# The last stage of a fused two-block transformer kernel: four places for split operands, and gates and gelus loaded in double pairs

## The chip, the cores and the metric

One core of a Trainium2 chip (trn2) runs the whole program. The metric is the device time in microseconds (us), the median of several runs. TensorE (PE) multiplies, VectorE (DVE), ScalarE (ACT) and GpSimd (POOL) do the elementwise work, SyncE (SP) issues most transfers, and 16 DMA engines move the data between the chip's memory and SBUF.

## The reference, cut to what matters

The reference is a chain of two transformer blocks over 512 tokens of width 1024. All but the end of the second block is untouched by the change. That end is a layer of 16384 small experts (`peer_ffn`): each token picks 8 x 16 experts, and its output is the sum of their rows of `v`, each weighted by a gelu of the token's product with the expert's row of `u` and by a gate.

```python
def peer_ffn(h, w_q, keys1, keys2, u, v):
    ...
    def chunk(args):
        h_c, e_c, g_c = args
        a = jnp.einsum('cd,ced->ce', h_c.astype(jnp.float32), u[e_c].astype(jnp.float32))
        act = jax.nn.gelu(a, approximate=False) * g_c
        return jnp.einsum('ce,ced->cd', act, v[e_c].astype(jnp.float32))
    ...
x = x + peer_ffn(rmsnorm_2(x, norm2_g[l]), w_peer_q[l], peer_keys1[l], peer_keys2[l],
                 peer_u[l], peer_v[l])
```

## The kernel before

**Two ways for the experts.** For 384 of the 512 tokens (TD = 384) the kernel takes no picks: it multiplies by all experts, with a gate of zero where a token has not picked one. The 16384 experts are 64 pairs (PAIRS) of 256, 2 x 128 each. In the stage before the last, the products with `u` are made, their gelu goes to DRAM (`gelu_dram`, 384 KB a pair), and the gates, built from one-hot products, go to `gates_dram`. The other 128 tokens go by gathers: 128 gathers (SLOTS) of rows of `v`, two a pair, which GpSimd issues and VectorE multiplies by a scalar and adds into two PSUM banks (`add_rows`, line 1849).

**The last stage.** For each pair p it computes out[384 tokens, 1024] += (gelu x gate)[256 experts, 384] transposed, times v[256 experts, 1024]. Multiplications keep float32 precision with operands that are split into a high half (rounded to fp32r) and a low half (the rest): high x high, low x high, high x low. So a pair is 2 (halves of its experts) x 3 (token blocks) x 2 (512 columns) x 3 = 36 matmuls of 128 x 128 by 512 (lines 906 to 908, `outputs_of`), added up in six PSUM banks over all 64 pairs.

**Who does what for pair p.**
- SP issues the loads: a slab of weights of 1 MB into one of two places of `raw` (`value_slab`, line 374, when the slab two before it is split), then the gelus (line 384) and the gates (line 386) of the pair into one of two places (`pair`, when the product two before is out). All go through one queue; the gathers have another.
- ACT makes the high half of the weights, `W_hi<-raw` (`high`, line 1330), when PE is through with the pair that had the place, p-2, and the high half of the operand, `B_hi<-arena` (`operand`, line 1337), for which there are two places as well.
- GpSimd makes the low half of the weights, `W_lo<-raw,W_hi` (`low_of`, line 408), and then issues two gathers (line 464); gather k has one of eight places, and waits until VectorE has added the row block of gather k-8.
- VectorE does, in this order: the product gelu x gate (`product_of`, line 1830), the two sums of pair p-2 (`add_rows`), the low half of the operand, `B_lo` (`low_of`, line 1839).
- PE waits for `slab_split` (the low half of the weights) and `act_lo_ready` (the low half of the operand), and releases places with `slab_used`.

The engines are in step through semaphores alone; each runs its own list in the order in which it was written. The counts that are waited for are multiples of the pair: `slab_used` counts all slabs since the start, so that `slab_used >= slab - 1` means that the slab two before is through. At the end the four blocks of 128 tokens are copied out of PSUM by ACT and VectorE in turn (`x_done`) and stored. The block of the gathered tokens is copied first, when all its sums are made.

## Time and profile before

| what | value |
|---|---|
| median of 3 runs | 2793.13 us (2790.08 to 2794.68) |
| profiled execution | 2801.39 us, its span 2799.6 us |
| TensorE clock granted, mean over the span | 0.964 of full |
| PE busy | 2585.7 us (92%) |
| GpSimd busy | 1798.3 us (64%) |
| VectorE busy | 1674.6 us (60%) |
| ACT busy | 726.0 us (26%) |
| DMA, mean over the span | 180 GB/s, 502.83 MB |
| last stage, first to last matmul | 2221.3 to 2793.6 us of the span |

The span runs from the first to the last instruction; the profiled execution is some 8 us longer than the median of the timed runs. A busy share over the whole span says little here, since the stages have different limits; the stretch from 2221 us on is the one that the change touches. Matmuls overlap in the records, so their pace is the distance between two starts, not the duration of one. Rows of the timeline give an instruction's start, its duration, and in brackets how long its engine had been idle before it and who ended that.

### The profile page before, as it was taken

To read this page: it belongs to the slowest core of one execution; us is meant where nothing else is said; L and a number is where in the kernel's file an instruction comes from. 1 tells how busy PE (TensorE), PEld (TensorE's weight loads), DVE (VectorE), ACT (ScalarE), POOL (GpSimd) and SP (SyncE) were. 2 spreads that over 40 slices of the span, in tenths; PEclk is the share of its full clock that TensorE was granted. 3 is DMA by queue.
4 is the path that set the end of the run, shared out by engine and by line. 5 is a ranking of instruction groups with operands and counts; after the bars stand their busy time and mean duration, and the time that the engine had idled before them with its cause. 6 is when DMAs were issued, how large, how long until landed. Compare 5 with 4: busy or idle time off the path is not lost.

```text
span 2799.6 us, 36306 instructions
## 1 busy us (share of the span) xinstructions
PE 2585.7 (92%) x12764; PEld 2159.1 (77%) x12764; DVE 1674.6 (60%) x3128; ACT 726.0 (26%) x1296; POOL 1798.3 (64%) x1315
## 2 busy tenths in 40 slices
PE   4989799999899998998889989999999999999998
PEld 2866578888686675677778889999999977777777
DVE  5457531111334224454449998878788388878887
ACT  4158310000222323433311011111112123322332
POOL 2746557676651252375656568998986778777786
PEclk8989899999998998999999999999999999999999
DMA  6224222222210011122123336899997899989897
GB/s 239 90 83 151 91 75 95 101 90 97 104 61 31 31 60 49 46 91 91 63 95 111 119 123 253 310 351 327 350 333 260 317 324 325 329 298 324 314 327 256
DMA packets 160500, 502.83 MB, mean 180 GB/s; under 512 B 12288, under 2 KB 79488, under 8 KB 128896
## 3 DMA queue, kind: packets, MB, share of 16 engines
q1 hardware_dynamic: 96432, 311.98, 31.8%
q0 software_dynamic: 36864, 134.23, 12.9%
q10 hardware_dynamic: 27088, 55.11, 5.2%
q8 instruction: 68, 1.11, 0.2%
q14 instruction: 48, 0.39, 0.0%
HBM read 448.84 MB, written 52.43 MB: 179 GB/s over the span
## 4 chain that ended last, share of the span: by engine, by line
PE 58%; DVE 13%; POOL 10%; DMA 9%; issue 5%; ACT 4%; SPq 0%; ACTq 0%; DVEq 0%; POOLq 0%
PE banks L546 8%; PE banks L548 8%; PE banks L547 8%; POOL W_lo L408 6%; DMA arena<-gates_dram 5%; PE banks L676 3%; PE banks L906 3%; PE banks L907 2%; PE banks L908 2%; PE banks L821 2%; PE banks L823 2%; PE banks L822 2%; PE banks L694 2%; PE banks L652 2%; PE banks L695 2%
## 5 line engine op out<-in xcount | busy, mean ns | idle before, releaser
L408 POOL TENSOR_TENSOR W_lo<-raw,W_hi 128x2048 fp32r<-128x2048 f32 x127 | 586.6, 4619 | 58.8 <-ACT W_hi L1330 53.2
L433 POOL TENSOR_TENSOR W_lo<-raw,W_hi 128x512 fp32r<-128x512 f32 x376 | 493.8, 1324 | 0.0
L436 POOL TENSOR_TENSOR beat<-zero 128x1 f32<-128x1 f32 x94 | 19.3, 205 | 650.8 <-PE banks L696 255.8
L821 PE MATMUL banks<-A_hi,W_hi 128*128 128x384 f32 x1024 | 380.3, 371 | 18.9 <-ACT B_plain L1258 17.9
L823 PE MATMUL banks<-A_hi,W_lo 128*128 128x384 f32 x1024 | 345.3, 337 | 0.0
L822 PE MATMUL banks<-A_lo,W_hi 128*128 128x384 f32 x1024 | 344.3, 336 | 0.0
L906 PE MATMUL banks<-W_hi,B_hi 128*128 128x512 f32 x768 | 306.2, 399 | 33.3 <-DVE B_lo L1839 33.3
L907 PE MATMUL banks<-W_hi,B_lo 128*128 128x512 f32 x768 | 304.6, 397 | 0.0
L908 PE MATMUL banks<-W_lo,B_hi 128*128 128x512 f32 x768 | 304.1, 396 | 0.0
L546 PE MATMUL banks<-A_hi,W_hi 128*128 128x512 f32 x680 | 265.8, 391 | 4.9 <-issue 4.9
L548 PE MATMUL banks<-A_hi,W_lo 128*128 128x512 f32 x680 | 264.7, 389 | 0.0
L547 PE MATMUL banks<-A_lo,W_hi 128*128 128x512 f32 x680 | 264.6, 389 | 0.0
L428 POOL CAST W_hi<-raw 128x512 fp32r<-128x512 f32 x376 | 248.5, 675 | 0.0
L821 PEld LDWEIGHTS banks<-A_hi,W_hi 128*128 128x128 f32 x1024 | 195.4, 191 | 20.7 <-issue 12.1
L906 PEld LDWEIGHTS banks<-W_hi,B_hi 128*128 128x128 f32 x768 | 147.6, 192 | 70.5 <-DVE B_lo L1839 39.3
L464 POOL DMA_INDIRECT arena<-v_rows,arena x128 | 158.3, 1237 | 66.3 <-DVE banks L1849 43.2
L1839 DVE TENSOR_TENSOR B_lo<-arena,B_hi 128x768 fp32r<-128x768 f32 x64 | 190.5, 2977 | 11.9 <-ACT B_hi L1337 11.8
L822 PEld LDWEIGHTS banks<-A_lo,W_hi 128*128 128x128 f32 x1024 | 195.6, 191 | 0.0
L823 PEld LDWEIGHTS banks<-A_hi,W_lo 128*128 128x128 f32 x1024 | 193.8, 189 | 0.0
L416 POOL CAST W_hi<-raw 128x2048 fp32r<-128x2048 f32 x65 | 123.7, 1904 | 108.5 <-PE banks L823 86.6
L1330 ACT ACTIVATE W_hi<-raw 128x2048 fp32r<-128x2048 f32 x62 | 118.7, 1914 | 281.3 <-PE banks L908 281.2
L1830 DVE TENSOR_TENSOR arena<-arena 128x768 f32<-128x768 f32 x64 | 132.2, 2066 | 79.4 <-DMA arena<-gates_dram 79.3
(259 smaller groups left out, 5541.6 us busy)
## 6 DMA issues: line engine op xcount, KB each, us to landing
raw<-weights SPq DMA_DIRECT2D x241, 1024.0 KB, 4.9
gelu_dram<-B_plain ACTq DMA_DIRECT2D x64, 384.0 KB
gates_dram<-arena ACTq DMA_DIRECT2D x48, 512.0 KB, 9.1
arena<-gelu_dram SPq DMA_DIRECT2D x64, 384.0 KB, 7.6
arena<-gates_dram SPq DMA_DIRECT2D x64, 384.0 KB, 10.2
W_plain<-weights SPq DMA_DIRECT2D x4, 1024.0 KB, 15.7
X<-x_t SPq DMA_DIRECT2D x1, 2048.0 KB, 14.3
arena<-v_rows,arena POOLq DMA_INDIRECT x128, 8.4
```

The source lines that it names most:

```text
L408: pool.tensor_tensor(W_lo[:, s % 2, :], raw[:, s % 2, :], W_hi[:, s % 2, :].bitcast(F32), ALU.subtract)\
L428: pool.tensor_copy(W_hi[:, j, cols], raw[:, j, cols]).then_inc(slab_half, 1)
L433: return pool.tensor_tensor(W_lo[:, j, cols], raw[:, j, cols], W_hi[:, j, cols].bitcast(F32), ALU.subtract)
L546: mm(to, lh, rh, start=i == 0, stop=False)
L547: mm(to, lh, rl, start=False, stop=False)
L548: last = mm(to, ll, rh, start=False, stop=i == n - 1)
L821: mm(to, lh, rh, start=k == 0, stop=False)
L822: mm(to, lh, rl, start=False, stop=False)
L823: last = mm(to, ll, rh, start=False, stop=k == KD - 1)
L906: mm(to, lh, rh, start=False, stop=False, skip_group_check=True)
L907: mm(to, ll, rh, start=False, stop=False, skip_group_check=True)
L908: return mm(to, lh, rl, start=False, stop=final and j == 1, skip_group_check=True)
```

## The change

The last stage gets four places where it had two, for the split weights and for the split operands: weights of pairs 0 and 1 of each four stay in `W_hi`/`W_lo`, those of 2 and 3 go to `B_hi`/`B_lo`; the operands move from `B_hi`/`B_lo` to `A_hi`/`A_lo`. The waits for `slab_used` allow four pairs in flight. Gelus and gates are loaded for two pairs in one transfer each, into two double places, and SP issues them ahead of the two slabs of weights that belong to them, when the product three before is out. The product has three places, and VectorE's order becomes low half of p, product of p+2, sums of p-1. ACT makes the high half of the weights of p before the operand of p-1, and waits for all stores of gelus before it starts. The loops of ACT and SP are written out; PE's has four pairs in its body.

```diff
--- before.py
+++ after.py
@@ -203,11 +203,16 @@
 
         gate_t = [(B_plain if i < 4 else B_lo_plain)[:, 4 + i % 4, :] for i in range(KD)]
 
-        gelu_in, g_in, prod = at(0, 2, 2 * TD), at(2048, 2, 2 * TD), at(4096, 2, 2 * TD)
+        gelu_in, g_in, prod = at(0, 2, 4 * TD), at(4 * 2 * TD, 2, 4 * TD), [at(16 * TD, 2 * TD), at(18 * TD, 2 * TD), at(16384, 2 * TD)]
         gelu_out = B_plain[:, 0:4, :]
         u_got = [(B_lo_plain[:, 2 * i:2 * i + 2, :] if i < 4 else B_plain[:, 2 * i - 4:2 * i - 2, :])
                  .rearrange("p a b -> p (a b)") for i in range(U_GOT)]
         v_got = [at(8192 + D * i, D) for i in range(V_GOT)]
+        v_first = (N_ADA + N_MID + PAIRS) % 2
+        v_hi = [W_hi[:, v_first, :], W_hi[:, 1 - v_first, :], *(B_hi[:, 4 * i:4 * i + 4, :].rearrange("p a b -> p (a b)")
+                                                                for i in range(2))]
+        v_lo = [W_lo[:, v_first, :], W_lo[:, 1 - v_first, :], *(B_lo[:, 4 * i:4 * i + 4, :].rearrange("p a b -> p (a b)")
+                                                                for i in range(2))]
         y_tok = X.rearrange("p (q a) b -> p q (a b)", q=QT)
 
 
@@ -373,28 +378,30 @@
                 sp.wait_ge(slab_split, s + (j + base - N_ADA - 1))
                 sp.dma_start(raw[:, slot, :], stream[s + (base + j), :, :]).then_inc(slab_loaded[slot], 16)
 
-            def pair(s, j):
-
-                if isinstance(s, int):
-                    sp.wait_ge(g_stored[j], 8 * STORES * GB)
-                    sp.wait_ge(g_stored[1 - j], 8 * STORES * GB)
+            def two_pairs(s, d):
+
+                if s + d:
+                    if s:
+                        sp.wait_ge(act_ready, s + 2 * d - 2)
                 else:
-                    sp.wait_ge(act_ready, s + (j - 1))
-                sp.wait_ge(gelu_stored[j], s * 8 + 16)
-                sp.dma_start(gelu_in[:, j, :], gelu_dram[s + j, :, :, :].rearrange("p i t -> p (i t)"))\
-                    .then_inc(pair_loaded[j], 16)
-                sp.dma_start(g_in[:, j, :].rearrange("p (q x) -> p q x", q=GB),
-                             g_dram[:, :, bass.ds(s * 2 + 2 * j, 2), :].rearrange("q p e t -> p q (e t)"))\
-                    .then_inc(pair_loaded[j], 16)
+                    for j in range(2):
+                        sp.wait_ge(g_stored[j], 8 * STORES * GB)
+                for j in range(2):
+                    sp.wait_ge(gelu_stored[j], s * 8 + (16 * d + 16))
+                sp.dma_start(gelu_in[:, d, :].rearrange("p (s x) -> p s x", s=2),
+                             gelu_dram[s + 2 * d:s + 2 * d + 2, :, :, :].rearrange("s p i t -> p s (i t)"))\
+                    .then_inc(pair_loaded[d], 16)
+                sp.dma_start(g_in[:, d, :].rearrange("p (q x) -> p q x", q=GB),
+                             g_dram[:, :, 2 * s + 4 * d:2 * s + 4 * d + 4, :].rearrange("q p e t -> p q (e t)"))\
+                    .then_inc(pair_loaded[d], 16)
 
             for j in range(2):
                 value_slab(0, j)
-            for j in range(2):
-                pair(0, j)
-            with sp.Fori(2, PAIRS - 1, 2) as s:
+            two_pairs(0, 0)
+            for s in range(2, PAIRS, 2):
+                two_pairs(s // 4 * 4, s // 2 % 2)
                 for j in range(2):
                     value_slab(s, j)
-                    pair(s, j)
             for n, q in enumerate((QT - 1, *range(QT - 1))):
                 sp.wait_ge(x_done, 2 * n + 2)
                 sp.dma_start(out[P * q:P * q + P, :], y_tok[:, q, :]).then_inc(stored, 16)
@@ -480,8 +487,10 @@
                 pool.wait_ge(g_stored[i], 8 * STORES * GB)
             for s in range(N_MID + PAIRS + 1, N_MID + 2 * PAIRS + 1):
                 if N_MID + PAIRS + 2 <= s < n:
-                    pool.wait_ge(v_half, s - (N_MID + PAIRS + 1))
-                    low_of(s)
+                    p = s - (N_MID + PAIRS)
+                    pool.wait_ge(v_half, p - 1)
+                    pool.tensor_tensor(v_lo[p % 4], raw[:, s % 2, :], v_hi[p % 4].bitcast(F32), ALU.subtract)\
+                        .then_inc(slab_split, 1)
                 k = V_GATHERS * (s - (N_MID + PAIRS + 1))
                 for i in range(k + V_GATHERS * V_AHEAD if k else 0, min(SLOTS, k + V_GATHERS * (V_AHEAD + 1))):
                     gather(i, v_got, v_rows, v_gathered, v_added)
@@ -894,15 +903,15 @@
                               skip_group_check=True)
                 last.then_inc(x_rows_ready, 1)
 
-            def outputs_of(s, odd, final=False):
-                slot = (N_ADA + N_MID + PAIRS + odd) % 2
-                pe.wait_ge(slab_split, s + (odd + N_MID + PAIRS + 1))
-                pe.wait_ge(act_lo_ready, s + (odd + 1))
+            def outputs_of(s, i, final=False):
+                pe.wait_ge(slab_split, s + (i + N_MID + PAIRS + 1))
+                pe.wait_ge(act_lo_ready, s + (i + 1))
 
                 def part(q, half, j):
                     to = two_banks[q][:, 512 * half:512 * half + 512]
-                    lh, ll = act_tile("B", 4 + 2 * odd + j, P * q, P)
-                    rh, rl = w_tile(slot, D * j + 512 * half, 512)
+                    lh, ll = act_tile("A", 2 * i + j, P * q, P)
+                    cols = slice(D * j + 512 * half, D * j + 512 * half + 512)
+                    rh, rl = v_hi[i][:, cols], v_lo[i][:, cols]
                     mm(to, lh, rh, start=False, stop=False, skip_group_check=True)
                     mm(to, ll, rh, start=False, stop=False, skip_group_check=True)
                     return mm(to, lh, rl, start=False, stop=final and j == 1, skip_group_check=True)
@@ -920,11 +929,11 @@
                                 last = part(q, half, j)
                     last.then_inc(slab_used, 1)
 
-            with pe.Fori(0, PAIRS - 3, 2) as s:
-                for odd in range(2):
-                    outputs_of(s, odd)
-            outputs_of(PAIRS - 2, 0)
-            outputs_of(PAIRS - 2, 1, final=True)
+            with pe.Fori(0, PAIRS - 7, 4) as s:
+                for i in range(4):
+                    outputs_of(s, i)
+            for i in range(4):
+                outputs_of(PAIRS - 4, i, final=i == 3)
 
 
         @block.scalar
@@ -1321,28 +1330,29 @@
             act.wait_ge(u_dotted, SLOTS)
             act.activation(dots, dots, ACT.Gelu).then_inc(dots_gelu, 1)
 
-            def high(s, j):
-
-                slab = s + (j + N_MID + PAIRS)
-                slot = (N_MID + PAIRS + j) % 2
-                act.wait_ge(slab_loaded[slot], s * 8 + (8 * (N_MID + PAIRS + j - slot + N_ADA - 4) + 16))
-                act.wait_ge(slab_used, slab - 1)
-                act.activation(W_hi[:, slot, :], raw[:, slot, :], ACT.Copy).then_inc(v_half, 1)
-
-            def operand(s, j):
-
-                act.wait_ge(act_ready, s + (j + 1))
-                if not isinstance(s, int):
-                    act.wait_ge(slab_used, s + (j + N_MID + PAIRS - 1))
-                act.activation(B_hi[:, 4 + 2 * j:6 + 2 * j, 0:TD], prod[:, j, :].rearrange("p (i t) -> p i t", i=2),
-                               ACT.Copy).then_inc(act_hi_ready, 1)
-
-            for j in range(2):
-                operand(0, j)
-            with act.Fori(2, PAIRS - 1, 2) as s:
-                for j in range(2):
-                    high(s, j)
-                    operand(s, j)
+            def high(p):
+
+                slab = p + N_MID + PAIRS
+                act.wait_ge(slab_loaded[slab % 2], 8 * (slab - slab % 2 + N_ADA - 4) + 16)
+                if p >= 4:
+                    act.wait_ge(slab_used, slab - 3)
+                act.activation(v_hi[p % 4], raw[:, slab % 2, :], ACT.Copy).then_inc(v_half, 1)
+
+            def operand(p):
+
+                act.wait_ge(act_ready, p + 1)
+                if p >= 4:
+                    act.wait_ge(slab_used, p + N_MID + PAIRS - 3)
+                act.activation(A_hi[:, 2 * (p % 4):2 * (p % 4) + 2, 0:TD],
+                               prod[p % 3].rearrange("p (i t) -> p i t", i=2), ACT.Copy).then_inc(act_hi_ready, 1)
+
+            for i in range(2):
+                act.wait_ge(gelu_stored[i], 8 * PAIRS)
+            operand(0)
+            for p in range(2, PAIRS):
+                high(p)
+                operand(p - 1)
+            operand(PAIRS - 1)
             act.wait_ge(x_rows_ready, QT)
             act.wait_ge(v_added, SLOTS)
             act.activation(y_tok[:, QT - 1, 0:512], bank[6][:, :], ACT.Copy).then_inc(x_done, 1)
@@ -1825,20 +1835,21 @@
 
             def product_of(p):
 
-                j = p % 2
-                dve.wait_ge(pair_loaded[j], 16 * (p - j) + 32)
-                dve.tensor_tensor(prod[:, j, :].rearrange("p (i q t) -> p i q t", i=2, q=GB),
-                                  gelu_in[:, j, :].rearrange("p (i q t) -> p i q t", i=2, q=GB),
-                                  g_in[:, j, :].rearrange("p (q i t) -> p i q t", i=2, q=GB), ALU.mult)\
-                    .then_inc(act_ready, 1)
+                d, j = p // 2 % 2, p % 2
+                dve.wait_ge(pair_loaded[d], 32 * (p // 4) + 32)
+                if p >= 3:
+                    dve.wait_ge(act_lo_ready, p - 2)
+                dve.tensor_tensor(prod[p % 3].rearrange("p (i q t) -> p i q t", i=2, q=GB),
+                                  gelu_in[:, d, 2 * TD * j:2 * TD * j + 2 * TD].rearrange("p (i q t) -> p i q t", i=2, q=GB),
+                                  g_in[:, d, :].rearrange("p (q i t) -> p i q t", i=4, q=GB)[:, 2 * j:2 * j + 2, :, :],
+                                  ALU.mult).then_inc(act_ready, 1)
 
             def low_of(p):
 
-                j = p % 2
                 dve.wait_ge(act_hi_ready, p + 1)
-                dve.tensor_tensor(B_lo[:, 4 + 2 * j:6 + 2 * j, 0:TD], prod[:, j, :].rearrange("p (i t) -> p i t", i=2),
-                                  B_hi[:, 4 + 2 * j:6 + 2 * j, 0:TD].bitcast(F32), ALU.subtract)\
-                    .then_inc(act_lo_ready, 1)
+                tiles = slice(2 * (p % 4), 2 * (p % 4) + 2)
+                dve.tensor_tensor(A_lo[:, tiles, 0:TD], prod[p % 3].rearrange("p (i t) -> p i t", i=2),
+                                  A_hi[:, tiles, 0:TD].bitcast(F32), ALU.subtract).then_inc(act_lo_ready, 1)
 
             def add_rows(p):
 
@@ -1851,15 +1862,17 @@
 
             dve.wait_ge(dots_gelu, 1)
             step(dve.tensor_tensor(dots, dots, gates, ALU.mult))
+            for p in range(2):
+                product_of(p)
             for p in range(PAIRS):
-                product_of(p)
-                if p == 2:
+                low_of(p)
+                if p + 2 < PAIRS:
+                    product_of(p + 2)
+                if p == 1:
                     dve.wait_ge(x_rows_ready, 1)
-                if p >= 2:
-                    add_rows(p - 2)
-                low_of(p)
-            for p in range(PAIRS - 2, PAIRS):
-                add_rows(p)
+                if p >= 1:
+                    add_rows(p - 1)
+            add_rows(PAIRS - 1)
             dve.wait_ge(x_rows_ready, QT)
             dve.wait_ge(v_added, SLOTS)
             dve.wait_ge(x_done, 1)
```

## Rows read from the trace of the kernel before

**Rows 1.** The page, part 2: mean busy share of the DMA engines in 40 slices.

```profile
DMA  6224222222210011122123336899997899989897
```

**Rows 2.** Grouped lines, 1750 to 2800 us: busy us, mean ns; idle before, releaser.

```profile
L408 POOL TENSOR_TENSOR W_lo<-raw,W_hi 128x2048 fp32r<-128x2048 f32 x107 | 494.5, 4622 | 57.2 <-ACT W_hi L1330 53.2
L906 PE MATMUL banks<-W_hi,B_hi 128*128 128x512 f32 x768 | 306.2, 399 | 33.3 <-DVE B_lo L1839 33.3
...
L1849 DVE SCALAR_TENSOR_TENSOR banks<-arena,banks 128x1024 f32<-128x1024 f32 x128 | 164.4, 1285 | 9.3 <-DMA arena<-v_rows,arena 2.7
...
L1330 ACT ACTIVATE W_hi<-raw 128x2048 fp32r<-128x2048 f32 x62 | 118.7, 1914 | 281.3 <-PE banks L908 281.2
```

**Rows 3.** Timeline of PE: start us, duration us, engine, line, [idle before].

```profile
2221.63 0.40 PE L907 MATMUL banks<-W_hi,B_lo 128*128 128x512 f32 x1
...
2245.66 0.39 PE L908 MATMUL banks<-W_lo,B_hi 128*128 128x512 f32 x1
...
2292.76 0.79 PE L906 MATMUL banks<-W_hi,B_hi 128*128 128x512 f32 x1 [2.80 <-DVE B_lo L1839]
2293.35 0.63 PE L907 MATMUL banks<-W_hi,B_lo 128*128 128x512 f32 x1
...
2793.61 0.39 PE L908 MATMUL banks<-W_lo,B_hi 128*128 128x512 f32 x1
```

**Rows 4.** Waits, 1850 to 2800 us: us in total, times, longest.

```profile
ACT W_hi L1330 <- PE banks L908: 281.2, 51, 9.6
...
POOL arena L464 <- DVE banks L1849: 43.2, 30, 2.5
...
PE banks L906 <- DVE B_lo L1839: 33.3, 14, 2.8
```

**Rows 5.** Windows: us, then busy us by engine, granted clock, DMA share, GB/s.

```profile
2296.00:2341.00 45.00, 45.00 (x199) 37.00 (x199) 38.02 (x21) 13.38 (x10) 36.29 (x16) 1.00 0.90 324
2341.00:2349.00 8.00, 5.20 (x19) 3.91 (x18) 7.79 (x7) 3.49 (x3) 5.27 (x4) 0.87 0.97 339
```

**Rows 6.** Timeline of VectorE at one of the waits.

```profile
2284.58 4.67 DVE L1830 TENSOR_TENSOR arena<-arena 128x768 f32<-128x768 f32 x1 [3.28 <-DMA arena<-gates_dram]
...
2291.75 0.95 DVE L1839 TENSOR_TENSOR B_lo<-arena,B_hi 128x768 fp32r<-128x768 f32 x1
```

**Rows 7.** Timeline of GpSimd: a gather that waits, and two subtractions in step.

```profile
2290.72 0.96 POOL L464 DMA_INDIRECT arena<-v_rows,arena  x1 [2.29 <-DVE banks L1849]
...
2312.96 4.61 POOL L408 TENSOR_TENSOR W_lo<-raw,W_hi 128x2048 fp32r<-128x2048 f32 x1 [0.84 <-ACT W_hi L1330]
...
2321.11 4.61 POOL L408 TENSOR_TENSOR W_lo<-raw,W_hi 128x2048 fp32r<-128x2048 f32 x1 [0.65 <-ACT W_hi L1330]
```

**Rows 8.** DMA of 2221 to 2790 us (five rows), 2320 to 2322, 2326 to 2328.

```profile
DMA packets 84738, 179.85 MB, mean 316 GB/s; under 512 B 5008, under 2 KB 52624, under 8 KB 76924
...
q1 hardware_dynamic: 66300, 112.67, 59.0%
q0 software_dynamic: 18432, 67.12, 30.2%
...
raw<-weights SPq DMA_DIRECT2D x61, 1024.0 KB, 6.8
...
arena<-gates_dram SPq DMA_DIRECT2D x61, 384.0 KB, 10.3
...
DMA packets 108, 0.80 MB, mean 399 GB/s; under 512 B 5, under 2 KB 5, under 8 KB 14
...
DMA packets 589, 0.53 MB, mean 264 GB/s; under 512 B 28, under 2 KB 554, under 8 KB 561
```

**Rows 9.** The stage's start: ACT's timeline, and the queue's packets in 2218 to 2220.

```profile
2219.40 0.84 ACT L1337 ACTIVATE B_hi<-arena 128x768 fp32r<-128x768 f32 x1 [6.01 <-DVE arena L1830]
...
q10 hardware_dynamic: 26, 0.04, 4.9%
```

**Rows 10.** The end: VectorE's last copy, 2795.84 to 2796.53 us.

```profile
2795.84 0.69 DVE L1870 COPY X<-banks 128x512 f32<-128x512 f32 x1 [0.79 <-ACT X L1352]
```

## The prediction: what the change does to the time

> **What bounds the kernel now.** The slices of the page come first: in the last eight, which hold the last stage, the DMA share stands at 8 and 9 tenths but for the very end, so the transfers are nearly full there [rows 1]. The grouped lines then give the size of the stage: three lines of 768 matmuls, 2304 in all, 36 for each of the 64 pairs [rows 2]. Their 390 ns overlap, so the pace is read from two starts in the timeline of PE: from the second matmul of the stage (2221.63) to the 108th (2245.66) there are 106 steps, 226.7 ns each [rows 3]. A pair is therefore worth 36 x 0.2267 = 8.16 us. From the second to the last matmul (2793.61) the trace shows 571.98 us for 2302 steps, which at 226.7 ns would be 521.9 us. So 50.1 us of this stage are not matmul work. That is the whole sum that the change can address.
>
> The waits tell what the 50.1 us are: PE waited 14 times for the low half of an activation operand (B_lo, VectorE), 33.3 us in all [rows 4]. Ten of the 14 are 2.80 or 2.81 us long and come every five or six pairs; one of 1.35 us is the start. The other 18 of the 50.1 us stand behind them: after a wait the granted clock falls to the lower of its two levels (1.2 GHz), and the matmuls take 0.63 us in place of 0.39 and start 0.43 us apart, as from 2293.35 on, behind the wait before 2292.76 [rows 3]; 6 to 14 such steps stand behind each of eight of the waits. In the windows the granted clock is 1.00 over 45 us without a wait and 0.87 in the 8 us around one [rows 5]. Every group of 0.43 us steps in this stage begins within 3 us of a wait: no wait, no slow group.
>
> What makes a wait is read from the other engines at 2284 to 2293. VectorE sat idle 3.28 us for the gates of its pair (they landed late), then the product took 4.67 us where the low half, of the same size, takes 0.95, since GpSimd was in its 4.62 us subtraction and VectorE's two-input operations on SBUF don't pass beside it. Then came the two row sums (2 x 1.29 and a handover, 2.67 us), which stand ahead of the low half in VectorE's order, and only then the low half, at 2291.75; PE starts at 2292.76 [rows 2, 3, 6]. The gates are late because they are asked for last of three transfers of a pair, and land 10.3 us after their issue (median), more than a pair's 8.16 us [rows 8]. The queues were not free to catch up: the two queues took 59.0% and 30.2% of the 16 engines over 569 us, 507.5 us of engine time. The 179.85 MB of that stretch are 62.4 pairs (1.05 MB of weights, two operands of 0.39, two gathers of 0.52: 2.88 MB), so a pair takes 8.13 us of all engines, against PE's 8.16 [rows 8]. And ACT, which splits the weights' high half, waited 281 us for PE to give a place back [rows 4]: with two places nothing can run ahead.
>
> **The change, part by part.** (1) *Four places for the split weights and for the operands.* The high half of pair p now waits for PE to be through with pair p-4, not p-2. Before, the weights' chain was 1.91 us (ACT) and 4.62 us (GpSimd) after PE's release [rows 2], 1.6 us less than the pair that hid it; now it has 8.16 x 2 = 16.3 us more. It removes no work. What it is worth hangs on whether the work ahead of PE runs faster than 8.16 us a pair, so each supplier is costed.
>
> GpSimd: from one subtraction (2312.96) to the next (2321.11) there are 8.15 us, of which it waited 0.65: 7.50 us of its own, two gathers included [rows 7]. ACT: 1.91 + 0.84 = 2.8 us [rows 2, 9]. VectorE: product 0.95, low half 0.95, two sums 2.67: 4.6 us, and one wait for GpSimd's port of up to 4.6. The load of a slab: two places in raw, so half of (landing 6.8 + 1.91 + 4.62) = 6.7 us [rows 2, 7, 8].
>
> (2) *Gates and gelus in double pairs.* 64 + 64 transfers become 32 + 32, with the same bytes. A row of gates was 2 x 64 floats, 512 B, 768 packets a pair; now it is 1024 B and 768 packets for two pairs. The price of a packet of 512 B: in 2326 to 2328, when 554 of the 589 packets were small ones, the engines moved 264 GB/s, where the weights' large packets in 2320 to 2322 ran at 399 GB/s, 24.9 B/ns an engine. Counting the two microseconds as full (32 engine-us), the 28 packets of 8 KB take 9.2 of them, which leaves 561 small ones in 22.8: 40 ns each, 1.92 us a pair. No row shows a packet of 1024 B. From below it costs no more than one of 512 B (40 ns, 0.96 us a pair); from above 40 + 21 ns, the second half at the large packets' rate (1.46 us a pair); above even that, no gain at all. I take 1.2, so a pair needs 8.13 - 0.7 = 7.4 us of the queues [rows 8].
>
> The Trainium skill ("DMA: Bandwidth & Descriptors", Specifications) puts the smallest transfer at line rate at 512 B; by that the gates are at full rate already and part (2) gives nothing but order. The 264 GB/s against 399 speak against it here. That case is rival A below.
>
> (3) *Order.* SP now asks for pairs P and P+1 before slab P, right behind slab P-1, when the product of P-3 is out. Product P comes in VectorE's order behind low half P-2. Walked through from the rows' durations, the request has 8.6 us to land behind one slab and beside two gathers while PE has no lead (3.4 MB at 385 GB/s: 8.8 us, so a product may be some tenths late), and 16 us or more once the lead is there. SP itself is not a bound: its issues cost 0.3 to 0.4 us, and behind its waits stand only weights that are two slabs away.
>
> (4) *VectorE and ACT in a new order.* low(p), product(p+2), then the sums of p-1. The sums no longer stand ahead of the low half that PE waits for: 2.67 us off that path. ACT now does the high half of p ahead of operand p-1, so the operand waits for slab p too: with a lead this costs nothing, without one it puts the low half about 9.3 us behind the release of slab p, plus GpSimd's subtraction if it starts first. The third product place costs nothing. The gathers of GpSimd wait for sums that now come behind a low half and a product. That is rival B and C.
>
> (5) *Start.* ACT waits for all gelu stores before the first operand. Operand 0 ran at 2219.40, once its product was out. Packets of the last store still ran in 2218 to 2220, and the pairs 2 and 3, now asked for at once (1.6 MB, some 4 us), stand beside it: 0 to 4 us later, I take 1.7 [rows 9]. The eight first gathers and the first slabs are as before. Walking pairs 2 to 7, each low half comes 3 to 4 us ahead of PE and GpSimd makes a pair in 8.0 us; for stalls left in this ramp I allow 3 us (0 to 8; one stall with its slow group costs some 4.1).
>
> (6) *End.* Before, ACT's first copy waited for VectorE's last sums, and the four pairs of copies ran on until 2796.53, 2.5 us behind the last matmul (2794.0). With the sums done earlier only one pair of copies (0.79 for ACT's with its handovers, 0.69 for VectorE's: 1.5 us) stands behind PE: 1.0 us less [rows 3, 10]. PE's body of four pairs and the unrolled ACT and SP cost nothing that a row shows: PE's idle time in the stage is named "B_lo" alone [rows 4].
>
> **The sum.** 50.1 removed, 1.7 and 3.0 back, 1.0 at the end: 46.4 us. Against the profiled execution (2801.4 us, of which 2799.6 is the span) that is 2755.0; the median of the runs, 2793.1, is 8.3 lower, and I take the difference over as it is: 2746.7.
>
> **The rivals.** *A: DMA is the bound.* If a 1024 B packet costs twice a 512 B packet, a pair stays at 8.13 us of engine time, or at 8.3 by the rate of the fullest window (339 GB/s at a share of 0.97 [rows 5], 349 GB/s for 2.88 MB). The stage is then 64 x 8.3 = 531 us in place of 522: 9 us worse, 2756. For it: the DMA slices at 9. Against: the two rates [rows 8], and a share of 0.90 between the waits [rows 5].
>
> *B: GpSimd and VectorE hold each other, now and then.* If a low half is late enough that the subtraction starts first, low (0.95), product (0.95) and first sum (1.29) come after it, and the gathers behind these: 4.6 + 0.95 + 0.95 + 1.29 + 1.38 (the second sum and its handover) + 0.96 (the last gather) = 10.1 us for that pair. The old trace has this form: GpSimd idle 2.29 us before a gather, for VectorE's sum [rows 7]. One such pair in three gives (10.1 + 2 x 7.5)/3 = 8.4 us a pair, 15 us more, and with the stalls' slow clock and handovers some 27: 2774. For: 43.2 us of such waits in 30 places before [rows 4], and the new order lengthens the chain. Against: in a stage paced by PE the low half starts while GpSimd still gathers, and the pattern falls back by itself.
>
> *C: slower.* The same lock in every pair, its place GpSimd's gathers behind VectorE's sums: 10.1 x 64 = 646 us against 572, that is 2867. It decides from the point where more than every second pair is of that kind ((10.1 + 7.5)/2 = 8.8, beside the 8.94 of before). For: operands asked of ACT only after the next slab. Against: after a late pair the next slab has long landed, so the next low half is early.
>
> *D: the change doesn't do what it says:* the lead never forms since raw still has two places. The stage keeps its waits: 2790. Against: 6.7 us for that loop.
>
> **Chances.** Forecast 0.58 (2740 to 2756), A 0.12, B 0.16, D 0.04, C 0.10. B reaches up to no change in a small part (0.01). The range 2740 to 2775 holds the forecast, A and half of B, 0.8. A measurement of this kernel can tell some 0.2% (5.6 us) from no change: faster 0.85, same 0.05, slower 0.10.
>
> **What would show it.** Right: PE's waits for the low half (now A_lo) under 5 us in sum and none after the first ten pairs, second to last matmul within 530 us, granted clock 1.00 throughout; ACT's high half waiting for PE with 5 us and more a time. Packets under 2 KB about half as many and the queues' share below 0.93 at a higher rate. Product wait for gates gone. For A: shares of 0.98 and more with PE waiting for the weights' low half. For B and C: GpSimd's gathers waiting for VectorE well over 43 us, and PE still waiting. The prediction is wrong if the DMA or GpSimd pace is above 8.16 us, or if the slow clock comes without waits.

## The result, and the profile after

The changed kernel takes 2781.1 us (median of 5, 2776.7 to 2784.4) against 2794.7 us (2790.1 to 2795.0): a ratio of 0.9948, 95% interval 0.9935 to 0.9960. It is faster by 13.6 us; 46 were forecast, and the time lies above the range.

The page of the changed kernel, slices and the busiest lines of the chain:

```profile
span 2779.3 us, 35520 instructions
...
PEclk8989999999998998999999999999999999999999
DMA  6224222222310011122222336899998899999996
...
DMA arena<-gates_dram 10%; PE banks L555 8%; PE banks L557 8%; PE banks L556 8%; PE banks L830 4%; PE banks L832 4%; PE banks L831 4%; DVE arena L1842 4%; PE banks L685 3%; PE banks L890 2%; PE banks L703 2%; PE banks L661 2%; PE banks L705 2%; PE banks L704 2%; PE banks L589 2%
```

The chain leads through the gates' transfer for 10% of the span, 5% before, and now through VectorE's product as well. The timeline of PE has the first matmul of the stage, one of its waits and the last matmul:

```profile
2223.92 0.77 PE L915 MATMUL banks<-W_hi,A_hi 128*128 128x512 f32 x1 [3.19 <-DVE A_lo L1851]
...
2608.14 0.39 PE L917 MATMUL banks<-W_lo,A_hi 128*128 128x512 f32 x1
2609.16 0.50 PE L915 MATMUL banks<-W_hi,A_hi 128*128 128x512 f32 x1 [0.64 <-DVE A_lo L1851]
...
2774.42 0.39 PE L917 MATMUL banks<-B_lo,A_hi 128*128 128x512 f32 x1
```

From the first to the last there are 550.5 us for 2303 steps; at 226.7 ns they would be 522.1, so 28.4 us are left over (below: the excess), where [rows 3] gave 50. (The spans differ by 20.3 us, more than the medians' 13.6: the profiled execution of the kernel before was 6.7 us above its median. Of the 20.3 the stage gives 21.8, a later first matmul takes 2.6, and the end gives 1.1.) The form has changed. Before, there were ten waits of 2.8 us, eight of them with the slow clock behind them. Now, from pair 21 on, there is a short wait before nearly every second pair (mostly 0.62 to 0.68 us idle, 1.0 us from start to start), and the granted clock is 1.00 from 2230 to 2730 us. The waits, us in total, times, longest:

```profile
ACT B_hi L1339 <- DMA raw<-weights: 182.4, 30, 10.8
ACT W_hi L1339 <- DMA raw<-weights: 181.4, 30, 16.1
DVE arena L1842 <- DMA arena<-gates_dram: 90.0, 27, 5.3
POOL arena L471 <- DVE banks L1860: 83.5, 59, 3.2
...
PE banks L915 <- DVE A_lo L1851: 22.4, 25, 3.2
```

Against [rows 4]: PE's waits fell from 33.3 to 22.4 us, but GpSimd's waits for VectorE's sums doubled from 43.2 to 83.5 us, and ACT waits for slabs that have not landed, where it waited for PE. PE's lead (from the end of a low half to the first matmul that needs it) was 6.4 us at pair 10 and 0.1 us at pair 21: it was used up, and the four places stayed half empty.

Why is in the timelines of one double pair. GpSimd:

```profile
2582.97 4.60 POOL L492 TENSOR_TENSOR B_lo<-raw,B_hi 128x2048 fp32r<-128x2048 f32 x1
2589.87 0.96 POOL L471 DMA_INDIRECT arena<-v_rows,arena  x1 [2.30 <-DVE banks L1860]
2591.26 1.40 POOL L471 DMA_INDIRECT arena<-v_rows,arena  x1 [0.43 <-DVE banks L1860]
2592.68 4.62 POOL L492 TENSOR_TENSOR W_lo<-raw,W_hi 128x2048 fp32r<-128x2048 f32 x1
2597.46 1.50 POOL L471 DMA_INDIRECT arena<-v_rows,arena  x1 [0.16 <-issue]
2599.26 0.94 POOL L471 DMA_INDIRECT arena<-v_rows,arena  x1 [0.30 <-issue]
2600.21 4.62 POOL L492 TENSOR_TENSOR W_lo<-raw,W_hi 128x2048 fp32r<-128x2048 f32 x1
```

VectorE (L1842 is the product, L1860 the sums, L1851 the low half):

```profile
2584.24 4.16 DVE L1842 TENSOR_TENSOR arena<-arena 128x768 f32<-128x768 f32 x1 [3.37 <-DMA arena<-gates_dram]
2588.32 2.67 DVE L1860 SCALAR_TENSOR_TENSOR banks<-arena,banks 128x1024 f32<-128x1024 f32 x2
2590.90 0.95 DVE L1851 TENSOR_TENSOR A_lo<-arena,A_hi 128x768 fp32r<-128x768 f32 x1
2591.77 0.95 DVE L1842 TENSOR_TENSOR arena<-arena 128x768 f32<-128x768 f32 x1
2592.64 2.68 DVE L1860 SCALAR_TENSOR_TENSOR banks<-arena,banks 128x1024 f32<-128x1024 f32 x2
2595.22 2.91 DVE L1851 TENSOR_TENSOR A_lo<-arena,A_hi 128x768 fp32r<-128x768 f32 x1
2601.70 3.95 DVE L1842 TENSOR_TENSOR arena<-arena 128x768 f32<-128x768 f32 x1 [3.57 <-DMA arena<-gates_dram]
```

And SP, which asks for the slabs (two issues in one row) and for the gates:

```profile
2588.47 0.47 SPq L394 DMA_DIRECT2D arena<-gates_dram  x1
2597.33 7.87 SPq L379 DMA_DIRECT2D raw<-weights  x2
2605.76 0.47 SPq L394 DMA_DIRECT2D arena<-gates_dram  x1
```

Gates asked for at 2588.47 are there at 2601.70, 13.2 us later; VectorE had been free for the product since 2598.13, 9.7 us after the request. By then GpSimd is in the subtraction that began at 2600.21, so the product takes 3.95 us instead of 0.95. The sums come behind the product, GpSimd's gathers behind the sums (idle 2.30 us), the next subtraction behind the gathers. From subtraction to subtraction it is 9.71 us, then 7.53, and so on: 17.26 us for two pairs, 8.63 a pair, against PE's 8.16. The pattern feeds itself: SP asks for the next gates behind a slab, and asks for that slab only when the subtraction two before it is done (2600.21 + 4.62; the second slab of the row is asked for at 2604.86, the gates at 2605.76), so a late subtraction also makes the next request late. From pair 7 to pair 21 PE lived on what lead there was, then it waited before nearly every second pair. What it waits for is the low half of p+1, and that stands in VectorE's list behind the product of p+2 and the sums.

### The profile page after: what moved, and what is told of

It reads as the page before. It is cut to its first block, busy times and chain, and to the rows that moved or that the text cites. A ratio compares the mean times of both kernels' runs of the same rounds, so it can differ in the third digit from the quotient of the medians.

```text
span 2779.3 us, 35520 instructions
## 1 busy us (share of the span) xinstructions
PE 2576.3 (93%) x12764; PEld 2150.7 (77%) x12764; DVE 1634.0 (59%) x3128; ACT 723.1 (26%) x1296; POOL 1787.6 (64%) x1315
## 4 chain that ended last, share of the span: by engine, by line
PE 59%; DVE 15%; DMA 15%; POOL 5%; issue 3%; ACT 3%; ACTq 0%; SPq 0%; DVEq 0%; POOLq 0%
DMA arena<-gates_dram 10%; PE banks L555 8%; PE banks L557 8%; PE banks L556 8%; PE banks L830 4%; PE banks L832 4%; PE banks L831 4%; DVE arena L1842 4%; PE banks L685 3%; PE banks L890 2%; PE banks L703 2%; PE banks L661 2%; PE banks L705 2%; PE banks L704 2%; PE banks L589 2%
## 5 line engine op out<-in xcount | busy, mean ns | idle before, releaser
L415 POOL TENSOR_TENSOR W_lo<-raw,W_hi 128x2048 fp32r<-128x2048 f32 x65 | 298.8, 4596 | 5.2
L471 POOL DMA_INDIRECT arena<-v_rows,arena x128 | 150.1, 1173 | 100.1 <-DVE banks L1860 83.5
L1842 DVE TENSOR_TENSOR arena<-arena 128x768 f32<-128x768 f32 x64 | 156.0, 2438 | 90.1 <-DMA arena<-gates_dram 90.0
L1860 DVE SCALAR_TENSOR_TENSOR banks<-arena,banks 128x1024 f32<-128x1024 f32 x128 | 164.3, 1284 | 9.5 <-DMA arena<-v_rows,arena 2.7
L915 PE MATMUL banks<-B_hi,A_hi 128*128 128x512 f32 x384 | 151.0, 393 | 11.9 <-DVE A_lo L1851 11.8
L915 PE MATMUL banks<-W_hi,A_hi 128*128 128x512 f32 x384 | 151.6, 395 | 10.6 <-DVE A_lo L1851 10.6
L1315 ACT ACTIVATE arena<-banks 128x512 f32<-128x512 f32 x96 | 57.4, 598 | 382.4 <-PE banks L890 283.9
L1815 DVE TENSOR_SCALAR arena<-banks,arena 128x128 f32<-128x128 f32 x384 | 133.4, 347 | 39.7 <-PE banks L890 21.6
L1816 DVE TENSOR_SCALAR arena<-banks,arena 128x128 f32<-128x128 f32 x384 | 154.6, 402 | 0.0
```

The source lines that it names most:

```text
L415: pool.tensor_tensor(W_lo[:, s % 2, :], raw[:, s % 2, :], W_hi[:, s % 2, :].bitcast(F32), ALU.subtract)\
L915: mm(to, lh, rh, start=False, stop=False, skip_group_check=True)
L1842: dve.tensor_tensor(prod[p % 3].rearrange("p (i q t) -> p i q t", i=2, q=GB), gelu_in[:, d, 2 * TD * j:2 * TD * j + 2 * TD].rearrange("p ( ...
L1860: dve.scalar_tensor_tensor(out=y_rows[:, :], in0=v_got[k % V_GOT], scalar=dots[:, k:k + 1], in1=y_rows[:, :], op0=ALU.mult, op1=ALU.add).t ...
```

## The experiments

The theory after the result, L (for lock: GpSimd's subtraction holds VectorE's product or low half back until it is done): late gates make the product fall into a subtraction, and because sums and gathers stand behind that product, GpSimd loses the 2.3 us with it; either the order or the lateness has to go. The rival, D: the transfers are the bound, and the order only decides who waits. All ratios are to the kernel before, timed beside each run, with their 95% intervals; the excess is that of the profiled execution, over the pace of 226.7 ns from the first to the last matmul.

**1. The sums ahead of the product.**

```diff
                 low_of(p)
-                if p + 2 < PAIRS:
-                    product_of(p + 2)
                 if p == 1:
                     dve.wait_ge(x_rows_ready, 1)
                 if p >= 1:
                     add_rows(p - 1)
+                if p + 2 < PAIRS:
+                    product_of(p + 2)
```

> The changed kernel with VectorE's order low(p), sums of p-1, product(p+2), in place of low(p), product(p+2), sums of p-1. Theory L (lock and queue): in the changed kernel every second product lands behind GpSimd's subtraction, and the sums and GpSimd's gathers stand behind that product; with the sums ahead of it GpSimd's wait of 2.3 us in every second pair goes, the two-pair cycle falls from 17.26 to about 16.3 us, and the time to 2765 (ratio to before 0.989 to 0.991). Theory D (transfers): the gates land 13.2 us after their issue because the DMA engines are full; the order of VectorE's work behind them changes nothing, ratio 0.994 to 0.996, PE still waits some 0.65 us in every second pair.

Measured: 2754.2 us, 0.9850 (0.9834 to 0.9867), excess 3.5 us. Two lines in another order are worth 27 us. L was right in direction and too low in size (it said 0.989 to 0.991); D's 0.994 is out. GpSimd's waits for the sums fell to 41.2 us and weren't gone: the long distance of 9.7 us between two subtractions now comes once in four pairs, (9.72 + 3 x 7.54)/4 = 8.09 us a pair, just under PE's 8.16. The gates are hardly late any more, though they are asked for at the same place:

```profile
POOL arena L471 <- DVE banks L1860: 41.2, 29, 2.5
...
DVE arena L1842 <- DMA arena<-gates_dram: 10.1, 15, 1.9
```

**2. Gathers two pairs ahead, not three.** `V_AHEAD = 3` becomes `V_AHEAD = 2` in the changed kernel, nothing else.

> The changed kernel with gathers issued two pairs ahead, not three (V_AHEAD = 2): a gather then needs the sums of one pair earlier, so GpSimd has no reason to wait for VectorE. Theory L: GpSimd's waits for the sums (83.5 us) fall to under 15 us, the cycle to 16.3 us a double pair, ratio 0.989 to 0.991. Theory D: the same bytes at the same share, ratio 0.994 to 0.996.

Measured: 2750.1 us, 0.9835 (0.9821 to 0.9849), excess 3.2 us. L was right in direction and again too low in size, D is out. GpSimd no longer waits for VectorE, and now ACT waits for PE, as was forecast of the change itself; here, and in run 7, the four places fill. With the same loads and the same order of VectorE, the first product of a double pair now comes 15 to 16 us after its gates' request, where it came after 9.7 us: part of the gates' lateness was made by the lost time itself.

```profile
ACT B_hi L1339 <- PE banks L917: 136.3, 25, 5.5
ACT W_hi L1339 <- PE banks L917: 128.2, 24, 5.5
```

**3. The four places alone.** The kernel before with `v_hi`/`v_lo`, the operands in `A_hi`/`A_lo` and the waits for p-4; SP's, VectorE's and ACT's order stay. ACT's wait for the gelu stores is in it. Of the edits, the one to ACT's high half:

```diff
-                act.wait_ge(slab_used, slab - 1)
-                act.activation(W_hi[:, slot, :], raw[:, slot, :], ACT.Copy).then_inc(v_half, 1)
+                if p >= 4:
+                    act.wait_ge(slab_used, slab - 3)
+                act.activation(v_hi[p % 4], raw[:, slab % 2, :], ACT.Copy).then_inc(v_half, 1)
```

> The kernel before with the four places for split weights and operands alone; single loads of gates and gelus behind their slab, and VectorE's and ACT's order as before. Theory L: the product still catches the subtraction and the low half still stands behind product and sums; the places give back only ACT's wait for PE, ratio 0.996 to 1.000. Theory D: 8.13 us a pair of engine time nearly fills 8.16, so the lead of two more pairs evens out the landings and most of the gain is here, ratio 0.990 to 0.995.

Measured: 2785.6 us, 0.9961 (0.9948 to 0.9975), excess 33.9 us, with 25 waits of PE. The places alone are worth some 11 us, at the lower end of L's range; the interval just reaches D's upper end too. GpSimd still waits 81.6 us for the sums.

**4. The double loads alone.** The kernel before with SP's new list (`two_pairs` ahead of the slabs) and the product reading from double places. Two places for weights and operands, the old order. SP's list, without the body of `two_pairs`, which is that of the change:

```diff
-            for j in range(2):
-                pair(0, j)
-            with sp.Fori(2, PAIRS - 1, 2) as s:
+            two_pairs(0, 0)
+            for s in range(2, PAIRS, 2):
+                two_pairs(s // 4 * 4, s // 2 % 2)
                 for j in range(2):
                     value_slab(s, j)
-                    pair(s, j)
```

> The kernel before with the double loads alone, asked for ahead of their slabs; two places for weights and operands, VectorE's and ACT's order as before. Theory L: the products of a double pair come early for one of two, so about half of the twelve waits of PE go: ratio 0.993 to 0.997. Theory D: packets of 1 KB save 0.24 us of engine time a pair, 15 us in 64 pairs, if the engines are the bound: 0.994; without four places the rest stays.

Measured: 2746.9 us, 0.9828 (0.9815 to 0.9842), excess 0.1 us, no wait of PE in the stage. Both theories missed: a part of the change is worth 50 us, nearly four times the whole. VectorE (three lines and the next product) and GpSimd in this kernel:

```profile
2574.28 0.95 DVE L1833 TENSOR_TENSOR arena<-arena 128x768 f32<-128x768 f32 x1
2575.15 2.67 DVE L1853 SCALAR_TENSOR_TENSOR banks<-arena,banks 128x1024 f32<-128x1024 f32 x2
2577.78 4.74 DVE L1843 TENSOR_TENSOR B_lo<-arena,B_hi 128x768 fp32r<-128x768 f32 x1
2582.45 0.95 DVE L1833 TENSOR_TENSOR arena<-arena 128x768 f32<-128x768 f32 x1
...
2573.69 1.50 POOL L466 DMA_INDIRECT arena<-v_rows,arena  x1
2575.49 0.94 POOL L466 DMA_INDIRECT arena<-v_rows,arena  x1 [0.30 <-issue]
2577.10 4.61 POOL L410 TENSOR_TENSOR W_lo<-raw,W_hi 128x2048 fp32r<-128x2048 f32 x1 [0.66 <-ACT W_hi L1332]
```

Here an operation is caught by the subtraction in every single pair (4.74 us for 0.95), yet nothing is lost. It is the low half, the last of VectorE's three steps: product and sums are out before it, so the gathers never wait, and it ends 0.8 us behind the subtraction, which PE needs anyway, and 0.5 us before PE comes to the pair.

**5. Single loads, asked for ahead of the slab.** In the kernel before, `pair(s, j)` and `value_slab(s, j)` change places in SP's loop.

> The kernel before, with one edit: SP asks for the gates and gelus of a pair (single loads, rows of 512 B) ahead of the pair's slab, not behind it. It parts the two things in the double loads: when they are asked for, and the size of their rows. If asking earlier is what freed 50 us with the double loads: ratio 0.983 to 0.987 here too, no wait of VectorE for gates. If the size of the rows does it: 0.997 to 1.003.

Measured: 2757.7 us, 0.9860 (0.9845 to 0.9875), excess 7.9 us, all of it from one wait of 4.8 us at pair 3 and the slow clock behind it. This is what the first expectation said. When the gates are asked for is thus worth 38 us; of the 11 us to run 4, 7.9 are this start. The 16 DMA engines were at 98% (64.6 and 33.5) from 2240 to 2740 us, and behind that one wait (it ends at 2249.89) PE did not wait:

```profile
DMA packets 81621, 173.12 MB, mean 346 GB/s; under 512 B 4813, under 2 KB 50893, under 8 KB 73930
...
q1 hardware_dynamic: 64337, 110.16, 64.6%
q0 software_dynamic: 17280, 62.92, 33.5%
```

**6. Double loads with rows of 512 B.** Run 4 with the gates of a double pair in two transfers.

> The double loads alone (two places, old order; ratio 0.983), but the gates of a double pair in two transfers with rows of 512 B, asked for at the same time. By the traces a row of 1 KB costs 65 ns and one of 512 B 40 ns, 0.24 us a pair of engine time; if only the time of asking matters: 0.982 to 0.985; if the 8.13 us a pair of the small rows bind against PE's 8.16: 0.986 to 0.995.

Measured: 2747.7 us, 0.9825 (0.9811 to 0.9838), excess 0.0 us: as run 4. The size of the rows is worth nothing in time that can be measured here. (At 65 and 40 ns the difference would be 0.36 us a pair, 384 x 65 ns against 768 x 40 ns on 16 engines, not the 0.24 of the expectations. The queues' time a pair, by their share from 2240 to 2740 us and the bytes moved in it, was 7.9 us here and 7.6 in run 4.) D falls with this and run 5.

**7. Four places and double loads in the old order.** Run 3 with run 4's loads; against the changed kernel, VectorE's list (the last two pairs' sums follow the loop), ACT's operand p behind the high half of p, and two product places.

```diff
-            for p in range(2):
+            for p in range(PAIRS):
                 product_of(p)
-            for p in range(PAIRS):
+                if p == 2:
+                    dve.wait_ge(x_rows_ready, 1)
+                if p >= 2:
+                    add_rows(p - 2)
                 low_of(p)
-                if p + 2 < PAIRS:
-                    product_of(p + 2)
-                if p == 1:
-                    dve.wait_ge(x_rows_ready, 1)
-                if p >= 1:
-                    add_rows(p - 1)
-            add_rows(PAIRS - 1)
+            for p in range(PAIRS - 2, PAIRS):
+                add_rows(p)
```

> Four places and double loads, with VectorE's and ACT's order and the two product places of the kernel before: the changed kernel but for the order. If the new order (product of p+2 ahead of the sums, operand behind the next high half) is what costs 34 us of the 50: 0.982 to 0.985, as with the double loads alone. If the four places do harm by themselves, since GpSimd's subtraction then runs as soon as a slab lands and meets VectorE's product more often: 0.988 to 0.996.

Measured: 2750.6 us, 0.9838 (0.9825 to 0.9852), excess 1.6 us, as the first expectation said. Here the lead does form, 16.8 us from pair 24 on against 0.5 us in run 4, and ACT waits for PE:

```profile
ACT B_hi L1339 <- PE banks L917: 117.9, 22, 5.5
ACT W_hi L1339 <- PE banks L917: 114.6, 21, 5.5
```

So the four places do no harm to the steady pace, and bring nothing beyond the double loads. The changed kernel differs from this one in VectorE's and ACT's order and the third product place, and is 0.011 slower: some 30 us.

**8. ACT's operand ahead of the next high half**, in the changed kernel.

```diff
             for p in range(2, PAIRS):
+                operand(p - 1)
                 high(p)
-                operand(p - 1)
```

> The changed kernel with ACT's order turned: operand p-1 ahead of the high half of p, so that the low half no longer waits for the next slab. If ACT's order makes the late low half: ratio 0.984 to 0.989. If only VectorE's order (product ahead of sums) counts: 0.993 to 0.996, the two-pair cycle of 17.26 us unchanged.

Measured: 2778.6 us, 0.9938 (0.9924 to 0.9951), excess 29.4 us, the same 17.26 us from wait to wait. ACT's order costs nothing that shows in the changed kernel; by run 1, some 27 of the 30 us belong to VectorE's. (In run 1, where that loss is gone, the low half waits 45.0 us in sum for the operand that ACT makes behind the next high half. What that costs there, and what the third product place does, was not tried by itself; together they can hold only the 3 us between runs 1 and 7.)

**9. The subtraction in four parts**, in the changed kernel: four instructions of 512 columns on GpSimd.

> The changed kernel with GpSimd's subtraction in four parts of 512 columns. If the late product is dear because it is caught behind a whole subtraction (4.6 us), it now gets in after at most one part (1.3 us): the long products (3.9 to 4.6 us, every second pair) fall to 2.3 us or less and PE's waits shrink by half or more, ratio 0.986 to 0.992, although the four parts take 0.7 us more of GpSimd a pair. If the lock is a side matter, the 0.7 us show: 0.996 to 1.01.

Measured: 2803.8 us, 1.0027 (1.0014 to 1.0040), excess 58.5 us. The first expectation fell. But for one early case the product isn't let in between the parts:

```profile
2571.83 5.02 POOL L494 TENSOR_TENSOR W_lo<-raw,W_hi 128x512 fp32r<-128x512 f32 x4
...
2572.43 5.25 DVE L1845 TENSOR_TENSOR arena<-arena 128x768 f32<-128x768 f32 x1 [2.70 <-DMA arena<-gates_dram]
```

It starts 0.6 us into the first part and ends 0.8 us behind the fourth; 30 of the 31 products of this run that took over 2 us beside a subtraction in parts end so. The one that got in, at 2237.26 us, took 2.06 us and ended 0.8 us behind a first part (the second part then took 2.03 us for 1.3); why that one did stays open. The four parts take 0.4 us more than the whole, and the two-pair cycle went from 17.26 to some 18.1 us, twice that: both subtractions of a double pair lie on the cycle, and each makes it longer by what it takes itself.

**10. Half of the gates' bytes**, in the changed kernel: three of six token blocks are loaded (after the first double pair), so its output isn't the reference's.

> The changed kernel, but only three of the six token blocks of the gates are loaded after the first double pair (0.2 MB less a pair), so the output is not the reference's. It parts the late gates from the lock: if the cycle starts with gates that land during a subtraction, earlier gates (by some 1.2 us a double pair and with a lower share) end it: 0.981 to 0.986, no wait for gates. If GpSimd and VectorE hold each other whenever the order allows it, the cycle stays: 0.992 to 0.996.

Measured: 2751.4 us, 0.9833 (0.9806 to 0.9859), excess 6.7 us. With less to carry the gates come in time for most products (32.4 us of waits for 90.0; "no wait" had been expected), the long distance comes once in four pairs, and PE's steady waits end in the bad order as well. So the loss needs three things together, and each taken away alone ends it: the late gates (this run), the product ahead of the sums (run 1), and gathers issued three pairs ahead, not two (run 2).

**11. The wait for the gelu stores behind operand 0**, in the changed kernel.

> The changed kernel with ACT's wait for the gelu stores behind operand 0, which doesn't write the places that the stores read. The distance from the last matmul of the stage before to the first of the last stage was 11.5 us in the changed kernel and 9.7 in the kernel before; it should be 9.7 to 10.2 here. The time itself shifts by less than one run can tell.

Measured in its trace: 9.7 us from the last matmul of the stage before to the first of the last stage; 11.5 in the changed kernel, 9.7 in the kernel before. The wait for the stores costs 1.8 us at the start. The one time taken, 2782.8 us, tells nothing at this size, and its early pairs had a longer wait (6.2 us at pair 3), so whether the 1.8 us reach the end stays open.

## Why the prediction was wrong, point by point

- *What bounds the kernel.* Right, and shown: 50 us over the pace of 8.16 us a pair, from gates that land late. Run 5 takes that cause alone away and with it 38 us; run 4 has PE at 226.7 ns from end to end. The slow clock did come with the waits: in run 4, without a wait, the granted clock is 1.00 from 2230 to 2730 us; in the kernel before it is 0.97.
- *(1), four places.* Their value was put on the supplier's pace, rightly, but the lead was used up, as that pace was 8.63 us (above the 8.16 that the prediction itself names as its sign of being wrong). GpSimd's own 7.50 us were right (7.53 in every second pair); what failed is that they were taken for its pace. And where the lead did form, 16.8 us in run 7, it was worth nothing beside run 4: the places were not what held the 46 us.
- *(2), rows of 1 KB.* Estimated 40 to 61 ns, and no gain as the outer end. Between 2594 and 2598 us of the changed kernel the first queue moved 473 packets, nearly all of 1 KB, in 47.8% of the engines: 65 ns each, above my upper end. The queues took 7.9 us a pair here (92.0% of the 500 us from 2240 to 2740, for 58.2 pairs) and 7.6 in run 4, not 7.4. None of it matters for the time (runs 4 and 6). The Trainium skill's line rate from 512 B up ("DMA: Bandwidth & Descriptors", Specifications) is not what the small windows show (12.8 and 15.8 B/ns an engine against 24.9); but its consequence, that part (2) gives nothing by size, came true for another reason, since the engines were not the bound.
- *(3), order of loads.* This is the first step that failed. The landing was put at 8.8 us, from 3.4 MB at 385 GB/s; it was 13.2. The prediction's own sizes of a slab, 1.6 MB of gates and gelus and two gathers make 3.65 MB, and at the 336 GB/s that the changed kernel moved from 2240 to 2740 us these alone need 10.9 us; even in runs 2 and 4, which lose nothing, the median landing is 11.3 us. The time left for it failed too: "16 us or more once the lead is there" was so in runs 2, 4 and 7 (15 to 16 us), but in the changed kernel VectorE came to the product after 9.7 us, since the lead was used up. A product "some tenths late" was in fact 3.6 us late and met the next subtraction.
- *(4), VectorE's order.* This is the step that cost 27 of the 30 us between the changed kernel and run 7. I wrote that the sums no longer stand ahead of the low half that PE waits for. They do: low half p+1 stands behind product p+2 and the sums of p-1, so PE's next operand waits for gates that it doesn't need. In the old order the product ahead of a low half is its own, and with double loads its gates have had 15 to 16 us to land (run 7), not 9.7.
- *(5), start.* 1.7 forecast, 1.8 measured. *Ramp:* 3 us allowed; pairs 3 and 7 waited 1.7 and 1.6 us, right.
- *(6), end.* 1.0 less forecast; from the last matmul's start to the end of the span it was 6.0 us and is 4.9: right.
- *Rivals.* A is refuted by runs 4 and 6. B was the case in what it costs, with its two numbers about right (10.1 and 7.5; measured 9.7 and 7.5), but its start was another, late gates and not a late low half, and its frequency was wrong: one pair in two, not in three. (8.63 - 8.16) x 64 is 30 us; the excess was 28.4. I held that the pattern falls back by itself. It does, in the pair that follows, and then the next double load, which is late again, starts it anew: with double loads the lateness comes once in every two pairs, and that is its period. B was given 0.16, although the walk had GpSimd at 8.0 us a pair, most of the way from 7.5 to 8.16. C did not come, D neither: the waits did change.

## What to carry to other kernels

When an engine's list is reordered, ask of each step whose data come last and what stands behind it: in this kernel the step that could be late, or be caught by the lock, did no harm once it stood behind what the other engines wait for (runs 1 and 4). Test the parts of a change alone; here the transfers' request time (two lines of SP's list) held 38 of 50 us, and a new order of VectorE's list gave 27 of the 50 back. And ask how long a transfer has from its request to its use, against how long it takes to land: 16 against 11 us in run 4, 9.7 against 13 in the changed kernel. The version to keep is run 4, double loads with the old order: 0.983 of the time before, faster than both kernels.

## What the runs showed of the hardware that I had not expected

- VectorE's operation hardly ever comes between two of GpSimd's: with the subtraction in four instructions of 1.3 us, a waiting product of 0.95 us took 5.25 us and ended 0.8 us behind the fourth (run 9; so did 30 of 31 such products, and one got in behind the first part). Cutting this work into parts did not open a gap to count on.
- Two queues that took 98% of the 16 engines (run 5) fed PE without a wait from 2250 us on, at 346 GB/s; the kernel before had waits at 91%. The share alone did not tell a bound.
- After waits of 0.65 us (the changed kernel) and of 1.5 us (run 9) the granted clock stayed at its upper level, 1.00 from 2230 to 2730 us; of the ten waits of 2.8 us in the kernel before, eight were followed by the lower one.
